# A transformer stack on one Trainium2 core: the neighbourhood attention's output projection in split form

## The chip, the cores and the metric

The program runs on one core of a Trainium2 chip, in one launch. The metric is the device time of that core in microseconds. Below, PE is the matmul engine (TensorE), DVE is VectorE, ACT is ScalarE, POOL is GpSimd, and SP is the queue that issues the weight loads.

## The reference, cut to what matters

A first block (S5 branch, gated branch, cross attention, feed-forward) is followed by a second one of two layers. Each of these layers has a mixer and a feed-forward part, dense in layer 0 and a mixture of eight experts in layer 1. 256 tokens, 1024 features. The change touches only the mixer, which is, cut down:

```python
def mixer_block(x, w_in, b_gate, rpb, sink, w_branch_na, w_branch_sw, w_out):
    proj = x @ w_in
    q_na, k_na, v_na, q_sw, k_sw, v_sw, gate_logits = jnp.split(proj, ...)
    y_na = neighbourhood_attention(q_na, k_na, v_na, rpb)      # 8 heads of 64
    y_sw = sliding_window_attention(rotary(q_sw), rotary(k_sw), v_sw, sink)   # 8 heads of 64
    y_na = y_na @ w_branch_na                                  # (256, 512) @ (512, 1024)
    y_sw = y_sw @ w_branch_sw
    g_na, g_sw = jnp.split(sigmoid(gate_logits + b_gate), 2, axis=-1)
    return (g_na * y_na + g_sw * y_sw) @ w_out
```

## The kernel before, in words

**Two forms of a matmul.** An fp32 product is one instruction in the program and two records in the trace. The split form writes each operand as a high part (rounded to fp32r by ACT) and a low part (operand minus high part, by DVE), and adds up three fp32r matmuls: high x high, high x low, low x high. Most weights are used in split form (`split_a`, L701, and `split_b`, L728). The two branch projections of a mixer, `bna` with the weight `w_na` and `bsw` with `w_sw`, are in fp32 by `form_a4` (L668), which reads the weights straight from the ring.

**Weights.** SP streams chunks of 128 x 2048 elements into a ring of 7 slots in the fixed order of `plan_chunks`; the first matmul of a chunk releases a slot (`chunk_used`). `split_plan` (L138) lists the chunks that are split and the PSUM unit each is used for. ACT makes the high part of the next one at each `wp_part` (L1362), DVE the low part at each `wp_rest` (L1819), into two buffers that alternate; part n waits until PE has finished the unit of part n-2. So the places of these calls in the two engines' programs are the schedule of the splits, written by hand.

**PSUM.** Every result is a unit in the list of `plan_units`, and unit n lies in bank n mod 8. PE opens a unit when the consumer of the unit eight before has freed that bank.

**The pair attention** (`pair_attention`: PE L771, ACT L1315, DVE L1781) handles 8 pairs of heads, 0 to 3 for the neighbourhood and 4 to 7 for the sliding window. The engines run it in step, each in program order, one iteration j per pair:
- PE: the scores of pair j+1 (L781), the eight transposes of pair j-1's probabilities (L794; they wait for `prob_ready` from DVE), half of a gate's projection (24 split matmuls, L709), and the output of pair j-1 (L806; it waits for ACT's copies of the transposes).
- ACT: the exponentials of pair j (L1327), two copies of pair j-1's transposes (L1335), at odd j a sigmoid gate (L1561) and one `wp_part` (L1372), and last the copy of output j-1 out of PSUM (L1341), which frees its unit. It goes to `onT` in region r_v for pairs 0 to 3 and to `osT` in r_zu for the others.
- DVE: bias and scale of pair j's scores (L1792), their maximum (L1796) and its negative (L1802), then the reciprocal of pair j-1's sums (L1810) and the product with it (L1812), which raises `prob_ready`; at j = 2, 4 and 6 one `wp_rest` (L1825).

Behind the loop PE runs four banks of `bna` and four of `bsw` (L675, eight products a bank), then the output projection from the merged and split sum (L721), for which it waits on DVE's L1830. DVE multiplies the banks of `bna` by the gate (L2161), those of `bsw` too (L2166), and adds them (L2170). ACT's `merged_high` (L1378) and DVE's `merged_rest` (L1830) split the sum. Mixer 0 is followed by the dense feed-forward part, mixer 1 by the experts.

Of the kernel before, what the change touches and what calls it, by code (L numbers as in the profile page):

```python
# [137 lines left out]
def split_plan():  # L138

    out = [((("k8", "w_" + n, i)), (n, i)) for n in ("out", "q", "xo") for i in range(4)]  # L140
    for m in range(2):
        units = [(f"projb{m}", i) for i in range(5)] + [(f"{n}{m}", i) for n in ("qk", "ga", "gb") for i in range(4)]
        out += [(("k8", f"w_in_{m}", i), unit) for i, unit in enumerate(units)]
        out += [(("k8", f"w_out_{m}", i), (f"out{m}", i) if i < 3 else (f"last{m}", TB - 1)) for i in range(4)]
    return out
# [102 lines left out]
def build(nc, a, out):  # L248
    with ExitStack() as ctx:
# [3 lines left out]
        def sem(name):  # L253
            return ctx.enter_context(nc.semaphore(name))
# [84 lines left out]
        def view(region, lo, size, pat, **kw):  # L339
            return region[:, lo:lo + size].rearrange(pat, **kw)  # L340
# [50 lines left out]
        v_na = view(r_v, 0, 1024, "p (b d) -> p b d", b=TB)  # L391
        onT = view(r_v, 1024, 1024, "p (k t) -> p k t", t=TOK)
        qsT = view(r_k, 0, 1024, "p (k t) -> p k t", t=TOK)
# [43 lines left out]
        m_split = sem("m_split")  # L437
        hf_high = sem("hf_high")
        acc_free = sem("acc_free")
        qk_roped = sem("qk_roped")  # L440
# [43 lines left out]
        def free_unit(last, u):  # L484
            last.then_inc(bank_free[UNIT_AT[u] % BANKS], 1)
# [137 lines left out]
        def _(pe):  # L623
# [70 lines left out]

            def split_chunk(chunk):

                n = SPLIT_AT[chunk]
                pe.wait_ge(wp_split, n + 1)
                return [w.rearrange("p (k c) -> p k c", k=KD) for w in wp_slot(n)]

# [323 lines left out]
            for m in range(2):  # L1024
# [45 lines left out]
                for c in range(2):  # L1070
                    form_a4(f"bna{m}", ("k4", f"w_na_{m}", c), onT, 2 * c)
                evacuated(pe, (f"at{m}_o", PAIR_N - 1))
# [172 lines left out]
        def _(act):  # L1245
# [69 lines left out]
            def pair_attention(name, dst_of, sink_of, between):  # L1315
                g0 = head0[name]
                for j in range(PAIR_N + 1):
# [20 lines left out]
                    if j >= 1:  # L1338
                        u = (name + "_o", j - 1)
                        take_unit(act, u)  # L1340
                        free_unit(nc.scalar.activation(dst_of(j - 1), bank(u)[:, 0:TOK], ACT.Copy), u)  # L1341

# [185 lines left out]
            for m in range(2):  # L1528
# [47 lines left out]
                def gate_b(j):  # L1576

                    if j < PAIR_N and j % 2 == 1:
                        gate(f"gb{m}", j // 2, gbT, 8)
                        wp_part()  # L1580

                pair_attention(f"at{m}", lambda j: (onT if j < 4 else osT)[:, j % 4, :],
                               lambda i: sink_col(m, i - 8) if i >= 8 else None, gate_b)
                merged_high(4 + 4 * m)
                for _ in range(2):
# [82 lines left out]
        def _(dve):  # L1668
# [111 lines left out]

            def pair_attention(name, bias_of, sink_of):  # L1781
                g0 = head0[name]
                for j in range(PAIR_N + 1):
                    if j < PAIR_N:
# [12 lines left out]
                        if sink_of(2 * j) is not None:  # L1797
# [3 lines left out]
                            link(last)  # L1801
                        V.tensor_scalar(negm[:, j % 2, :], mx[:, j % 2, :], -1.0, None, ALU.mult).then_inc(negm_ready, 1)  # L1802
                    if j >= 1:
                        g = g0 + j - 1
# [327 lines left out]
            for m in range(2):  # L2132
# [18 lines left out]
                for _ in range(7):  # L2151
                    wp_rest()
                dve.wait_ge(loads["nab"], 16 * (m + 1))
                pair_attention(f"at{m}", lambda i: nabias[:, i, :, :] if i < 8 else swmask,
                               lambda i: sink_col(m, i - 8) if i >= 8 else None)
                wp_rest()
                evacuated(dve, (f"gb{m}", 3))
                for i in range(4):
                    take_unit(dve, (f"bna{m}", i))
                    gs = gaT[:, 2 * i:2 * i + 2, :]  # L2160
                    last = V.tensor_tensor(gs, gs, halves(bank((f"bna{m}", i))), ALU.mult)  # L2161
                    free_unit(last, (f"bna{m}", i))
                for i in range(4):
                    take_unit(dve, (f"bsw{m}", i))
# [315 lines left out]
```

## Time and profile before

| | |
|---|---|
| median of 3 runs | 2272.61 us (2268.06 to 2275.58) |
| the profiled execution | 2271.9 us |
| its span, first to last instruction | 2270.1 us |
| PE busy | 94% |
| PE weight loads busy | 83% |
| DVE busy | 69% |
| ACT busy | 53% |
| mean granted clock of PE | 0.972 |

The two pair attentions lie at 704 to 763 us (mixer 0) and 1113 to 1173 us (mixer 1), and the branch projections behind each take some 28 us. PE's records overlap one another, so the cost of a matmul in a row of equal ones is read from start to start, not from its duration. The bracket at the end of a timeline row is the idle time of the engine before it, and who ended it.

### The profile page before, as it was taken

The page shows a single profiled execution, that of the slowest core. Times are in us where ns is not written, and L with a number is a line of the kernel's source. Part 1 is how long each engine was busy: PE and PEld are TensorE (multiplying, and loading weights), DVE is VectorE, ACT ScalarE, POOL GpSimd, SP SyncE. Part 2 cuts the span into 40 slices and gives each one's busy share as a digit, 9 for nine tenths or more (in the row PEclk, how much of TensorE's full clock was granted, in tenths as well). Part 3 has the DMA queues.
Part 4 walks back from the last instruction along what each step waited for, and adds up shares of the span by engine and source line. Part 5 has one row for each costly group of instructions (what it writes and reads, how often), then busy time and mean ns, then how long its engine had stood idle before and what let it go on. Part 6 is the DMA issues. An engine that isn't in the chain of part 4 may idle for free.

```text
span 2270.1 us, 33147 instructions
## 1 busy us (share of the span) xinstructions
PE 2142.9 (94%) x12590; PEld 1875.5 (83%) x12590; DVE 1572.9 (69%) x1749; ACT 1195.3 (53%) x1215; POOL 9.8 (0%) x22
## 2 busy tenths in 40 slices
PE   7999988899898889998988999999999999999997
PEld 7888877799797789998877788888888888888885
DVE  8677343544636454454555888989898989899897
ACT  3200233333437433343552677777777777677774
POOL 0000000000000000000000000000000000000000
PEclk9999989899999989999998899999999999999998
DMA  7343432355463245555323698989898989989884
GB/s 300 140 149 111 147 117 97 122 186 185 157 246 117 93 149 186 186 186 201 134 89 116 271 371 344 367 345 367 341 365 341 367 350 362 371 336 370 351 357 161
DMA packets 76446, 542.02 MB, mean 239 GB/s; under 512 B 9152, under 2 KB 9296, under 8 KB 11968
## 3 DMA queue, kind: packets, MB, share of 16 engines
q1 hardware_dynamic: 72144, 524.32, 59.9%
q0 software_dynamic: 2080, 10.40, 1.2%
q10 hardware_dynamic: 2128, 5.93, 0.7%
q8 instruction: 73, 1.20, 0.2%
q14 instruction: 21, 0.17, 0.0%
HBM read 539.57 MB, written 1.05 MB: 238 GB/s over the span
## 4 chain that ended last, share of the span: by engine, by line
PE 88%; DVE 5%; ACT 4%; issue 1%; DMA 0%; DVEq 0%; ACTq 0%
PE psum L1178 13%; PE psum L822 11%; PE psum L1155 9%; PE psum L1159 9%; PE psum L1158 9%; PE psum L662 7%; PE psum L721 6%; PE psum L709 6%; PE psum L835 4%; PE psum L675 3%; PE psum L688 2%; PE psum L1121 2%; PE psum L1167 1%; ACT wp_h L1372 1%; PE psum L979 1%
## 5 line engine op out<-in xcount | busy, mean ns | idle before, releaser
L2210 DVE TENSOR_TENSOR w_l<-ring,w_h 128x2048 fp32r<-128x2048 f32 x338 | 773.2, 2290 | 115.5 <-ACT w_h L1358 108.9
L1358 ACT ACTIVATE w_h<-ring 128x2048 fp32r<-128x2048 f32 x338 | 647.5, 1916 | 138.9 <-PE psum L1155 95.4
L1155 PE MATMUL psum<-w_h,xe_h 128*128 128x512 f32 x896 | 359.8, 402 | 2.4 <-DVE xe_l L2294 2.4
L1159 PE MATMUL psum<-w_h,xe_l 128*128 128x512 f32 x896 | 350.6, 391 | 0.0
L1158 PE MATMUL psum<-w_l,xe_h 128*128 128x512 f32 x896 | 350.2, 391 | 0.0
L1851 DVE TENSOR_TENSOR wf_l<-ring,wf_h 128x2048 fp32r<-128x2048 f32 x66 | 151.2, 2291 | 156.5 <-ACT wf_h L1349 156.5
L1825 DVE TENSOR_TENSOR wp_l<-ring,wp_h 128x2048 fp32r<-128x2048 f32 x52 | 119.1, 2291 | 163.8 <-ACT wp_h L1372 163.8
L822 PE MATMUL psum<-xf_h,wf_h 128*128 128x256 f32 x704 | 200.9, 285 | 4.3 <-DVE xf_l L1843 2.4
L822 PE MATMUL psum<-xf_l,wf_h 128*128 128x256 f32 x704 | 200.6, 285 | 0.0
L822 PE MATMUL psum<-xf_h,wf_l 128*128 128x256 f32 x704 | 200.5, 285 | 0.0
L1155 PEld LDWEIGHTS psum<-w_h,xe_h 128*128 128x128 f32 x896 | 168.6, 188 | 38.2 <-DVE w_l L2210 3.9
L1159 PEld LDWEIGHTS psum<-w_h,xe_l 128*128 128x128 f32 x896 | 168.6, 188 | 36.2
L1158 PEld LDWEIGHTS psum<-w_l,xe_h 128*128 128x128 f32 x896 | 169.1, 189 | 32.3
L1349 ACT ACTIVATE wf_h<-ring 128x2048 fp32r<-128x2048 f32 x66 | 125.9, 1910 | 113.9 <-PE psum L835 58.5
L1372 ACT ACTIVATE wp_h<-ring 128x2048 fp32r<-128x2048 f32 x52 | 99.4, 1914 | 148.1 <-PE psum L721 78.3
L822 PEld LDWEIGHTS psum<-xf_h,wf_h 128*128 128x128 f32 x704 | 136.5, 194 | 5.8 <-DVE xf_l L1843 2.8
L1178 PE MATMUL psum<-w_h,eT_h 128*128 128x512 f32 x448 | 140.0, 394 | 0.0
L721 PE MATMUL psum<-wp_h,xf_h 128*128 128x256 f32 x384 | 114.5, 298 | 25.8 <-DVE xf_l L1859 12.9
L1178 PE MATMUL psum<-w_h,eT_l 128*128 128x512 f32 x448 | 138.4, 390 | 0.0
L1178 PE MATMUL psum<-w_l,eT_h 128*128 128x512 f32 x448 | 138.3, 390 | 0.0
L822 PEld LDWEIGHTS psum<-xf_l,wf_h 128*128 128x128 f32 x704 | 136.7, 194 | 0.7
L822 PEld LDWEIGHTS psum<-xf_h,wf_l 128*128 128x128 f32 x704 | 136.6, 194 | 0.0
(371 smaller groups left out, 3713.1 us busy)
## 6 DMA issues: line engine op xcount, KB each, us to landing
ring<-in_stream SPq DMA_DIRECT2D x499, 1024.0 KB, 5.8
big<-in_bc POOLq DMA_DIRECT2D x11, 512.0 KB, 7.6
big<-in_na_bias POOLq DMA_DIRECT2D x2, 2048.0 KB, 8.8
h<-in_x SPq DMA_DIRECT2D x2, 512.0 KB, 4.2
big<-in_mem ACTq DMA_DIRECT2D x1, 1024.0 KB, 12.2
big<-in_s_c ACTq DMA_DIRECT2D x1, 1024.0 KB, 13.2
r_k<-in_sgu_ln ACTq DMA_DIRECT2D x1, 1024.0 KB, 17.8
out_dram<-ysum ACTq DMA_DIRECT2D x1, 1024.0 KB, 4.0
```

The source lines that it names most:

```text
L662: last = nc.tensor.matmul(bank(unit)[:, j * TOK:(j + 1) * TOK], w[:, k, j * P:(j + 1) * P], act_T[:, k, :], start=(k == 0), stop=(k == KD ...
L709: last = nc.tensor.matmul(bank(unit)[:, j * TOK:(j + 1) * TOK], w[:, k, j * P:(j + 1) * P], x[:, k, :], start=(k == i == 0), stop=(k == KD ...
L721: last = nc.tensor.matmul(bank(unit)[:, at * 256:(at + 1) * 256], x[:, k, b * P:(b + 1) * P], w[:, k, :], start=(k == i == 0), stop=(k == ...
L822: last = nc.tensor.matmul(psum[:, ff_bank(name, b), j * TOK:(j + 1) * TOK], w[:, k, j * P:(j + 1) * P], x[:, k, :], start=(k == i == 0), s ...
L1155: first = nc.tensor.matmul(out, xe_h[:, k, :], wh[:, i, :], start=(k == 0), stop=False)
L1158: nc.tensor.matmul(out, xe_h[:, k, :], wl[:, i, :], start=False, stop=False)
L1159: last = nc.tensor.matmul(out, xe_l[:, k, :], wh[:, i, :], start=False, stop=(k == KD - 1))
L1178: last = nc.tensor.matmul(psum[:, 4 + c, :], x[:, s % 2, k, :], w[:, k, c * 512:(c + 1) * 512], start=(s == 0 and k == n == 0), stop=(s == ...
L1349: nc.scalar.activation(wf_h[:, n % SPLITS, :], ring[:, at % SLOTS, :], ACT.Copy).then_inc(wf_high, 1)
L1358: nc.scalar.activation(high, src, ACT.Copy).then_inc(w_high, 1)
L1851: V.tensor_tensor(wf_l[:, n % SPLITS, :], ring[:, at % SLOTS, :], wf_h[:, n % SPLITS, :].bitcast(F32), ALU.subtract).then_inc(wf_split, 1)
L2210: V.tensor_tensor(low, src, high.bitcast(F32), ALU.subtract).then_inc(w_split, 1)
```

## The change

- `bna` goes through the new `split_a4`, three fp32r matmuls for each fp32 product, on the split weight `w_na` and the split attention output. `split_plan` gets the two chunks of `w_na` behind those of the gates.
- The attention output of pairs 0 to 3 is split where it leaves PSUM: ACT's copy now writes the high part `on_h` (in a free half slot of `wf_l`) and raises `on_high`; DVE's new `on_rest` takes the low part `on_l` (in `hf_l`) from the same PSUM unit, and frees the unit instead of ACT.
- `on_rest` for pair j-2 stands in DVE's iterations j = 2 to 5, behind the negated maximum and before the reciprocal of pair j-1.
- ACT makes two more weight parts per mixer behind the loop and before `merged_high`. DVE makes the two low parts behind the second and the fourth bank of `bna`.

```diff
--- before.py
+++ after.py
@@ -141,6 +141,7 @@
     for m in range(2):
         units = [(f"projb{m}", i) for i in range(5)] + [(f"{n}{m}", i) for n in ("qk", "ga", "gb") for i in range(4)]
         out += [(("k8", f"w_in_{m}", i), unit) for i, unit in enumerate(units)]
+        out += [(("k4", f"w_na_{m}", c), (f"bna{m}", 2 * c + 1)) for c in range(2)]
         out += [(("k8", f"w_out_{m}", i), (f"out{m}", i) if i < 3 else (f"last{m}", TB - 1)) for i in range(4)]
     return out
 
@@ -389,7 +390,8 @@
         qnT = view(r_zu, 0, 1024, "p (k t) -> p k t", t=TOK)
         knT = view(r_zu, 1024, 1024, "p (k t) -> p k t", t=TOK)
         v_na = view(r_v, 0, 1024, "p (b d) -> p b d", b=TB)
-        onT = view(r_v, 1024, 1024, "p (k t) -> p k t", t=TOK)
+        on_h = wf_l[:, 1, 1024:2048].rearrange("p (k t) -> p k t", t=TOK)
+        on_l = hf_l.rearrange("p a b t -> p (a b) t")
         qsT = view(r_k, 0, 1024, "p (k t) -> p k t", t=TOK)
         ksT = r_k[:, 1024:1280]
         v_sw = view(r_k, 1280, 256, "p (b d) -> p b d", b=TB)
@@ -436,6 +438,7 @@
         wp_split = sem("wp_split")
         m_split = sem("m_split")
         hf_high = sem("hf_high")
+        on_high = sem("on_high")
         acc_free = sem("acc_free")
         qk_roped = sem("qk_roped")
         rexp_in = sem("rexp_in")
@@ -692,11 +695,26 @@
                             release(last, chunk)
                 close_unit(last, unit)
 
-            def split_chunk(chunk):
+            def split_chunk(chunk, k=KD):
 
                 n = SPLIT_AT[chunk]
                 pe.wait_ge(wp_split, n + 1)
-                return [w.rearrange("p (k c) -> p k c", k=KD) for w in wp_slot(n)]
+                return [w.rearrange("p (k c) -> p k c", k=k) for w in wp_slot(n)]
+
+            def split_a4(name, chunk, x_h, x_l, u0):
+
+                wh, wl = split_chunk(chunk, 4)
+                for u in range(2):
+                    open_unit(pe, (name, u0 + u))
+                    for j in range(2):
+                        at = slice((2 * u + j) * P, (2 * u + j + 1) * P)
+                        for k in range(4):
+                            for i, (w, x) in enumerate(((wh, x_h), (wh, x_l), (wl, x_h))):
+                                last = nc.tensor.matmul(bank((name, u0 + u))[:, j * TOK:(j + 1) * TOK], w[:, k, at],
+                                                        x[:, k, :], start=(k == i == 0), stop=(k == 3 and i == 2))
+                                if i == u == j == k == 0:
+                                    release(last, chunk)
+                    close_unit(last, (name, u0 + u))
 
             def split_a(unit, chunk, tiles=(0, 1)):
 
@@ -1068,7 +1086,7 @@
                                half_gate)
                 evacuated(pe, (f"at{m}_o", 3))
                 for c in range(2):
-                    form_a4(f"bna{m}", ("k4", f"w_na_{m}", c), onT, 2 * c)
+                    split_a4(f"bna{m}", ("k4", f"w_na_{m}", c), on_h, on_l, 2 * c)
                 evacuated(pe, (f"at{m}_o", PAIR_N - 1))
                 for c in range(2):
                     form_a4(f"bsw{m}", ("k4", f"w_sw_{m}", c), osT, 2 * c)
@@ -1338,7 +1356,11 @@
                     if j >= 1:
                         u = (name + "_o", j - 1)
                         take_unit(act, u)
-                        free_unit(nc.scalar.activation(dst_of(j - 1), bank(u)[:, 0:TOK], ACT.Copy), u)
+                        last = nc.scalar.activation(dst_of(j - 1), bank(u)[:, 0:TOK], ACT.Copy)
+                        if j - 1 < 4:
+                            last.then_inc(on_high, 1)
+                        else:
+                            free_unit(last, u)
 
             def wf_part(name, n):
 
@@ -1579,8 +1601,10 @@
                         gate(f"gb{m}", j // 2, gbT, 8)
                         wp_part()
 
-                pair_attention(f"at{m}", lambda j: (onT if j < 4 else osT)[:, j % 4, :],
+                pair_attention(f"at{m}", lambda j: (on_h if j < 4 else osT)[:, j % 4, :],
                                lambda i: sink_col(m, i - 8) if i >= 8 else None, gate_b)
+                for _ in range(2):
+                    wp_part()
                 merged_high(4 + 4 * m)
                 for _ in range(2):
                     wp_part()
@@ -1778,7 +1802,15 @@
                     if i >= 2:
                         xf_rest_of((name + "_o", i - 2), "x_o", i - 2)
 
-            def pair_attention(name, bias_of, sink_of):
+            def on_rest(m, j):
+
+                u = (f"at{m}_o", j)
+                take_unit(dve, u)
+                dve.wait_ge(on_high, 4 * m + j + 1)
+                last = V.tensor_tensor(on_l[:, j, :], bank(u)[:, 0:TOK], on_h[:, j, :].bitcast(F32), ALU.subtract)
+                free_unit(last, u)
+
+            def pair_attention(name, bias_of, sink_of, mixer):
                 g0 = head0[name]
                 for j in range(PAIR_N + 1):
                     if j < PAIR_N:
@@ -1800,6 +1832,8 @@
                                 last = V.tensor_scalar(m, m, sink_of(2 * j + hd), None, ALU.max)
                             link(last)
                         V.tensor_scalar(negm[:, j % 2, :], mx[:, j % 2, :], -1.0, None, ALU.mult).then_inc(negm_ready, 1)
+                    if 2 <= j < 6:
+                        on_rest(mixer, j - 2)
                     if j >= 1:
                         g = g0 + j - 1
                         dve.wait_ge(exp_ready, g + 1)
@@ -2152,7 +2186,7 @@
                     wp_rest()
                 dve.wait_ge(loads["nab"], 16 * (m + 1))
                 pair_attention(f"at{m}", lambda i: nabias[:, i, :, :] if i < 8 else swmask,
-                               lambda i: sink_col(m, i - 8) if i >= 8 else None)
+                               lambda i: sink_col(m, i - 8) if i >= 8 else None, m)
                 wp_rest()
                 evacuated(dve, (f"gb{m}", 3))
                 for i in range(4):
@@ -2160,6 +2194,8 @@
                     gs = gaT[:, 2 * i:2 * i + 2, :]
                     last = V.tensor_tensor(gs, gs, halves(bank((f"bna{m}", i))), ALU.mult)
                     free_unit(last, (f"bna{m}", i))
+                    if i % 2 == 1:
+                        wp_rest()
                 for i in range(4):
                     take_unit(dve, (f"bsw{m}", i))
                     gs = gbT[:, 2 * i:2 * i + 2, :]
```

In the rows of the program below, `hf_l<-psum,wf_l` is `on_rest`. This is DVE in mixer 0 before, iterations 2 and 3 of the pair attention:

```order
L1792 SCALAR_TENSOR_TENSOR r_zv<-psum,big 128x512 x2
L1796 TENSOR_REDUCE mx<-r_zv 128x4
L1802 TENSOR_SCALAR negm<-mx 128x4
L1810 RECIPROCAL rsum<-ssum 128x4
L1812 TENSOR_TENSOR uT<-uT,rsum 128x1024
L1825 TENSOR_TENSOR wp_l<-ring,wp_h 128x2048
L1792 SCALAR_TENSOR_TENSOR uT<-psum,big 128x512 x2
L1796 TENSOR_REDUCE mx<-uT 128x4
L1802 TENSOR_SCALAR negm<-mx 128x4
L1810 RECIPROCAL rsum<-ssum 128x4
```

and now:

```order
L1824 SCALAR_TENSOR_TENSOR r_zv<-psum,big 128x512 x2
L1828 TENSOR_REDUCE mx<-r_zv 128x4
L1834 TENSOR_SCALAR negm<-mx 128x4
L1810 TENSOR_TENSOR hf_l<-psum,wf_l 128x256
L1844 RECIPROCAL rsum<-ssum 128x4
L1846 TENSOR_TENSOR uT<-uT,rsum 128x1024
L1859 TENSOR_TENSOR wp_l<-ring,wp_h 128x2048
L1824 SCALAR_TENSOR_TENSOR uT<-psum,big 128x512 x2
L1828 TENSOR_REDUCE mx<-uT 128x4
L1834 TENSOR_SCALAR negm<-mx 128x4
L1810 TENSOR_TENSOR hf_l<-psum,wf_l 128x256
L1844 RECIPROCAL rsum<-ssum 128x4
```

One subtraction more stands in each of iterations 2 to 5, between the negated maximum and the reciprocal. The rest of the order is the same.

DVE behind mixer 0's pair attention, before:

```order
L1812 TENSOR_TENSOR uT<-uT,rsum 128x1024
L1825 TENSOR_TENSOR wp_l<-ring,wp_h 128x2048
L2161 TENSOR_TENSOR r_ga<-r_ga,psum 128x512 x4
L2166 TENSOR_TENSOR r_gb<-r_gb,psum 128x512
L2170 TENSOR_TENSOR r_ga<-r_ga,r_gb 128x512
```

and now (L1859 is `wp_rest`, L2195 the multiplication of a bank of `bna` by the gate, L2202 that of `bsw`):

```order
L1846 TENSOR_TENSOR uT<-uT,rsum 128x1024
L1859 TENSOR_TENSOR wp_l<-ring,wp_h 128x2048
L2195 TENSOR_TENSOR r_ga<-r_ga,psum 128x512 x2
L1859 TENSOR_TENSOR wp_l<-ring,wp_h 128x2048
L2195 TENSOR_TENSOR r_ga<-r_ga,psum 128x512 x2
L1859 TENSOR_TENSOR wp_l<-ring,wp_h 128x2048
L2202 TENSOR_TENSOR r_gb<-r_gb,psum 128x512
L2206 TENSOR_TENSOR r_ga<-r_ga,r_gb 128x512
```

The four multiplications of `bna` are now in twos, each two with a low part of an output weight behind it. The low part ahead of them belongs to `w_na` now, and to an output weight before.

ACT from the last output copy on, before:

```order
L1335 ACTIVATE r_zv<-psum 128x512 x2
L1341 ACTIVATE r_zu<-psum 128x256
L1378 ACTIVATE xf_h<-r_ga 128x512 x4
L1372 ACTIVATE wp_h<-ring 128x2048 x2
L1262 ACT_TABLE_LOAD
```

and now (L1400 is `merged_high`):

```order
L1353 ACTIVATE r_zv<-psum 128x512 x2
L1359 ACTIVATE r_zu<-psum 128x256
L1394 ACTIVATE wp_h<-ring 128x2048 x2
L1400 ACTIVATE xf_h<-r_ga 128x512 x4
L1394 ACTIVATE wp_h<-ring 128x2048 x2
L1280 ACT_TABLE_LOAD
```

Two high parts have come in ahead of `merged_high`.

## Rows read from the trace of the kernel before

**Rows 1.** The page, parts 1 and 4: busy time by engine; the chain by engine.
```profile
PE 2142.9 (94%) x12590; PEld 1875.5 (83%) x12590; DVE 1572.9 (69%) x1749; ACT 1195.3 (53%) x1215; POOL 9.8 (0%) x22
...
PE 88%; DVE 5%; ACT 4%; issue 1%; DMA 0%; DVEq 0%; ACTq 0%
```

**Rows 2.** Waits of PE, 1110 to 1205: us in total, times, longest us.
```profile
PE psum L806 <- ACT r_zv L1335: 7.1, 4, 2.2
...
PE psum L721 <- DVE xf_l L1830: 2.9, 1, 2.9
```

**Rows 3.** Timeline of DVE, mixer 1's neighbourhood projection: start, us, operation, idle before.
```profile
1180.88 0.69 DVE L2161 TENSOR_TENSOR r_ga<-r_ga,psum 128x512 f32<-128x512 f32 x1 [2.69 <-PE psum L675]
...
1187.78 0.69 DVE L2161 TENSOR_TENSOR r_ga<-r_ga,psum 128x512 f32<-128x512 f32 x1 [2.76 <-PE psum L675]
```

**Rows 4.** Timeline of PE in mixer 1's pair attention.
```profile
1126.92 1.14 PE L781 MATMUL psum<-r_zu 64*128 64x256 f32 x8
1127.98 1.09 PE L794 MATMUL psum<-ident,uT 128*128 128x128 f32 x8
1128.83 0.36 PE L709 MATMUL psum<-xf_h,wp_h 128*128 128x256 f32 x1
1129.04 0.28 PE L709 MATMUL psum<-xf_l,wp_h 128*128 128x256 f32 x1
...
1131.66 0.28 PE L709 MATMUL psum<-xf_h,wp_l 128*128 128x256 f32 x1
1133.38 1.08 PE L806 MATMUL psum<-r_zv,r_v 128*64 128x256 f32 x8 [1.44 <-ACT r_zv L1335]
...
1135.46 0.76 PE L794 MATMUL psum<-ident,r_zv 128*128 128x128 f32 x5
...
1141.51 0.76 PE L794 MATMUL psum<-ident,uT 128*128 128x128 f32 x5
...
1147.19 1.08 PE L806 MATMUL psum<-r_zv,r_v 128*64 128x256 f32 x8 [1.73 <-ACT r_zv L1335]
...
1149.27 0.98 PE L794 MATMUL psum<-ident,r_zv 128*128 128x128 f32 x7
...
1171.15 1.98 PE L806 MATMUL psum<-r_zv,r_k 128*64 128x256 f32 x8 [2.23 <-ACT r_zv L1335]
```

**Rows 5.** Timeline of DVE, last output projection: 128x256 operation that reads PSUM.
```profile
1226.49 0.42 DVE L2190 SCALAR_TENSOR_TENSOR h<-h,psum 128x256 f32<-128x256 f32 x1 [1.94 <-PE psum L721]
```

**Rows 6.** Timeline of DVE in mixer 1's pair attention, iteration 2.
```profile
1125.80 0.17 DVE L1810 RECIPROCAL rsum<-ssum 128x4 f32<-128x4 f32 x1
1126.01 1.22 DVE L1812 TENSOR_TENSOR uT<-uT,rsum 128x1024 f32<-128x1024 f32 x1
1128.68 2.29 DVE L1825 TENSOR_TENSOR wp_l<-ring,wp_h 128x2048 fp32r<-128x2048 f32 x1 [1.46 <-ACT wp_h L1372]
1130.89 1.28 DVE L1792 SCALAR_TENSOR_TENSOR uT<-psum,big 128x512 f32<-128x512 f32 x2
```

**Rows 7.** Timeline of ACT in mixer 1's pair attention.
```profile
1126.74 1.91 ACT L1372 ACTIVATE wp_h<-ring 128x2048 fp32r<-128x2048 f32 x1
1128.54 0.38 ACT L1341 ACTIVATE r_v<-psum 128x256 f32<-128x256 f32 x1
...
1134.50 0.39 ACT L1341 ACTIVATE r_v<-psum 128x256 f32<-128x256 f32 x1 [1.22 <-PE psum L806]
...
1141.99 0.38 ACT L1341 ACTIVATE r_v<-psum 128x256 f32<-128x256 f32 x1
```

**Rows 8.** Windows around two gaps of PE; the column behind POOL is the granted clock.
```profile
700.00:704.50 4.50, 1.52 (x14) 1.30 (x13) 2.03 (x1) 3.95 (x7) 0.00 (x0) 1.00 0.00 0
704.50:707.00 2.50, 2.48 (x20) 2.17 (x21) 1.53 (x3) 1.22 (x1) 0.00 (x0) 1.00 0.03 7
1109.60:1113.10 3.50, 0.51 (x7) 0.30 (x5) 2.07 (x1) 3.48 (x7) 0.00 (x0) 0.97 0.00 0
1113.10:1116.50 3.40, 3.40 (x16) 2.69 (x16) 1.49 (x3) 1.17 (x1) 0.00 (x0) 0.53 0.00 0
```

## The prediction

> **What bounds the kernel.** I began with the page's busy shares and its chain. TensorE (PE) is busy 94% of the span and carries 88% of the chain that ended last [rows 1]: a microsecond taken from PE counts in full, and so does a microsecond by which PE is made to wait. Then I asked what PE waits for in mixer 1's attention and projections [rows 2], and read that stretch on PE, VectorE (DVE) and ScalarE (ACT). Mixer 0 has the same schedule to within some tenths of a microsecond, so each term counts twice. PE's waits in the pair attention are for ACT's copies of the transposed probabilities, 7.1 us in four pieces, and one of 2.9 us stands before the output projection. The attention is thus a loop in which PE, DVE and ACT hand work round with little to spare. The change makes one projection cheaper on PE, and puts one more step into that loop.
>
> **1. The projection.** DVE takes one finished bank of it every 3.45 us (1180.88 to 1187.78 is two banks) [rows 3]. A bank holds 8 products of 128x128 by 256 columns, so one fp32 product costs 3.45 / 8 = 0.431 us. In the split form it is three matmuls; 23 of these start between 1129.04 and 1131.66, so 2.62 / 22 = 0.119 us each [rows 4], and 24 in a bank are 2.87 us. The gain is 0.58 us a bank, over four banks and two mixers **-4.6 us**, all of it on the path.
> By these rows an fp32 product costs 3.6 split matmuls. The Trainium skill (FP8 and Floating Point Precision, "TensorE Precision Notes") counts four passes for true fp32. With four the gain would be 64 x 0.119 = 7.6 us, and the sum 3 us lower; the rows decide.
>
> **2. The low half of each output, on DVE.** New in DVE's pair iterations 2 to 5 is a subtraction that waits for the output unit of pair j-2 and for ACT's copy of it. It stands in front of the reciprocal and the product that PE needs for its next transposes. DVE runs in order, so they wait too. For its own length I take the 0.42 us of the 128x256 row from PSUM [rows 5]; the bounds are the reciprocal's 0.17 [rows 6] and the 0.69 of twice the width [rows 3].
> - *Iteration 2.* Today the reciprocal starts at 1125.80, the product at 1126.01 and ends at 1127.23 [rows 6], and PE transposes at 1127.98, right behind the scores of 1126.92 [rows 4]. ACT's copy of output 0 comes only behind a gate and a 1.91 us weight split: 1128.54 + 0.38 = 1128.92 [rows 7]. The subtraction then runs to 1129.35, reciprocal and product take 0.21 + 1.22 = 1.43, and PE transposes at 1130.8: 2.8 late. PE idles from the end of the scores, 1128.06, for 2.7 us.
> - *Iteration 3.* PE's gate half starts 0.85 behind the transposes and lasts 24 x 0.12 = 2.9 us, so output 1 starts at 1134.6 instead of 1133.38, where it had waited 1.44 for ACT [rows 4]: part of the delay is swallowed. ACT's copy starts 1.12 behind (1134.50 today [rows 7]), ends near 1136.15, and with 0.42 + 1.43 the product is ready at 1138.0. PE transposes then, not at 1135.46 [rows 4]: 2.6 late. DVE's own scores work starts 2.0 late (behind the rest that followed the product) and would be ready before.
> - *Iteration 4.* All is 2.6 late on arrival. ACT's copy of output 2, again behind a gate and a split, ends at 1141.99 + 0.38 + 2.6 = 1145.0 [rows 7]; + 1.85 gives 1146.85. The transposes come there instead of at 1141.51 [rows 4]: 5.3 late.
> - *Iteration 5.* Output 3 starts at 1146.85 + 0.85 + 2.9 = 1150.6 where it was 1147.19 after 1.73 of waiting; copied 1152.1, transposes near 1154.0 to 1154.5 instead of 1149.27 [rows 4]: 5.0 late, 5.2 as middle.
>
> The last four iterations have no subtraction and run as today. They don't win the delay back, since PE, ACT and DVE have all been pushed by it. So **+5.2 us per mixer, +10.4 us**. With 0.17 in place of 0.42 in four serial places it is 2.0 less over both mixers, with 0.69 it is 2.2 more.
>
> **3. Two more splits per mixer, 1.91 on ACT and 2.29 on DVE each** [rows 6, 7]. During the attention their number is the same as now: the last two split the neighbourhood weights where the first two output weights were split. Those come behind the second and the fourth projection bank. DVE sits idle 2.7 us before every bank there [rows 3]. Behind the fourth bank ACT and DVE need 1.9 + 2.3 = 4.2 us, and the next bank is full after 3.45, so DVE takes it 0.8 late; a bank of the second projection costs DVE some 2.1 of its 3.45 us, so it has caught up one bank on. PE needs the first of these weights only after four such banks and 2.9 us more. Cost **0**; were that cover gone, it would be at most 2.3 us per mixer before the output projection.
>
> **4. Banks, ring, queues: 0.** An output's bank is freed by DVE, some 3 us later than by ACT, and is opened again eight units on. No DMA is issued; the ring's slots are released by the same first matmuls in the same order, and the weights now read early lie before those that were read at that time. SP only shifts with PE.
>
> **5. The clock.** PE now idles 2.7 us before the transposes of pairs 1 and 3, four times over both mixers. Idle PE has been followed by the lower level in these rows, though not always: 0.51 busy of 3.50 and then a granted clock of 0.53 over the next 3.4 us; the same gap in mixer 0 (1.52 of 4.50), then 1.00 [rows 8]; 2.23 us idle before the last output, whose eight records then took 1.98 where others take 1.08 [rows 4]. At the lower level (1.2 instead of 2.4 GHz) PE does half, so a stretch of 3.4 us costs up to 1.7 us, and here it falls on transposes, gate and output, which are on the path. Bounds are 0 and 4 x 1.7 = 6.8; I take two of four: **+3.4 us**. The Trainium skill (TensorE: Matmul & The Clock Gate, "HAM oscillation — how this bites in real kernels") warns only of gaps longer than these. By it this term is 0 and the sum +5.8; the row with 2.23 us idle speaks against it.
>
> **Sum:** -4.6 + 10.4 + 0 + 0 + 3.4 = **+9.2 us**. On the profiled execution's 2271.9 us that gives 2281.1; the median of the runs is 0.7 higher, within their spread of 7.5. I say 2281.
>
> **Rivals.**
> - *A, the forecast:* DVE's in-order wait plus one or more clock drops, 2281 (+7.5 with one, +12.6 with four).
> - *B, the same wait, the clock stays up:* +5.8, 2277.7. For it: the gap of some 3 us in mixer 0 did no harm. Against: the same gap in mixer 1, and one of 2.23, did. 0.3% is 6.8 us here, about what a measurement of this kernel can tell from no change, so this counts as no change.
> - *C, the splits behind the projection aren't covered:* DVE falls behind in the second projection, and PE's 2.9 us wait before the output projection [rows 2] grows by up to 2.3 per mixer: 2281 + 4.6 = 2286. Against it are DVE's 2.7 us gaps.
> - *D, the other side, the copy is there in time:* if ACT had output j-2 copied when DVE gets there, the subtraction would cost DVE 0.42 where it has slack, and the -4.6 would stand alone: 2267.3. It decides at 1125.8, and the copy lands at 1128.92, 3.1 too late; output 1's lands at 1134.88, and the transposes of 1135.46 need DVE to begin its last 1.43 us by 1134.0. To be faster by over 0.3% the fp32 products would also have to cost more than measured.
>
> **How the numbers follow.** Chances: A 0.57, B 0.29, C 0.06, D 0.08. Slower by over 0.3% is A and C, 0.63; within 0.3% is B and most of D, 0.34; faster 0.03. The range goes from B less the spread of a median, some 3 us, to four clock drops (2284.5) with the longer subtraction and the same spread: 2275 to 2289.
>
> **What would show it.** In the changed profile: DVE idle before the subtraction, ended by ACT's copy, about 3 us in iterations 2 and 4 and less in 3 and 5; PE idle before the transposes of pairs 1 and 3 near 2.7 us, ended by DVE's product; scores of pair 0 to the first projection matmul 5 us longer; projection banks 2.87 us apart, not 3.45; the wait before the output projection still 2.9. I am wrong if DVE finds the copy done, if the later iterations win back the delay, or if the output projection waits longer.

## The result, and the profile after

The changed kernel takes 2279.57 us (median of 6 runs, 2277.97 to 2283.92). The kernel before, run beside it, takes 2273.15 us (6 runs). The ratio is 1.0035, with a 95% interval of 1.0019 to 1.0051: slower by 6.4 us in the medians, 8 us by the ratio. The profiled execution is the slowest of the six, 2283.92 us with a span of 2282.1, against 2271.9 and 2270.1 before. So the two traces lie 12 us apart, more than the medians do, and some of that has to be something that isn't in every execution.

The page's busy times, and its chain by engine (compare [rows 1]):

```profile
PE 2144.2 (94%) x12654; PEld 1879.3 (82%) x12654; DVE 1585.2 (69%) x1761; ACT 1202.9 (53%) x1219; POOL 9.8 (0%) x22
...
PE 89%; DVE 6%; ACT 3%; issue 1%; DMA 0%; DVEq 0%; ACTq 0%
```

PE is busy 1.3 us more, though its work has become less, and DVE 12.3 us more. Nothing here tells where 12 us went. The waits of PE in mixer 1 do (us in total, times, longest; compare [rows 2]):

```profile
PE psum L812 <- DVE uT L1846: 5.5, 2, 2.8
PE psum L812 <- DVE r_zv L1846: 4.9, 4, 1.5
PE psum L824 <- ACT r_zv L1353: 4.0, 2, 2.2
PE psum L799 <- issue: 3.0, 1, 3.0
PE psum L739 <- DVE xf_l L1864: 2.9, 1, 2.9
```

L812 are the transposes, L824 the outputs, L739 the output projection. PE waited 7.1 us for ACT's copies before the outputs, and it waits 4.0 now. In their place come 10.4 us of waiting for DVE's product before the transposes, where the kernel before had 2.0:

```profile
PE psum L794 <- DVE r_zv L1812: 2.0, 2, 1.2
```

So PE waits 8.4 us more for DVE and 3.1 less for ACT, 5.3 in all. The wait before the output projection is 2.9 us, as it was.

DVE's timeline in mixer 1's loop, iteration 2 whole and the subtraction (L1810) of the next three (compare [rows 6]):

```profile
1134.83 0.17 DVE L1834 TENSOR_SCALAR negm<-mx 128x4 f32<-128x4 f32 x1
1138.13 0.42 DVE L1810 TENSOR_TENSOR hf_l<-psum,wf_l 128x256 fp32r<-128x256 f32 x1 [3.14 <-ACT wf_l L1359]
1138.47 0.17 DVE L1844 RECIPROCAL rsum<-ssum 128x4 f32<-128x4 f32 x1
1138.68 1.22 DVE L1846 TENSOR_TENSOR uT<-uT,rsum 128x1024 f32<-128x1024 f32 x1
...
1145.46 0.42 DVE L1810 TENSOR_TENSOR hf_l<-psum,wf_l 128x256 fp32r<-128x256 f32 x1 [0.70 <-ACT wf_l L1359]
...
1154.30 0.42 DVE L1810 TENSOR_TENSOR hf_l<-psum,wf_l 128x256 fp32r<-128x256 f32 x1 [2.74 <-ACT wf_l L1359]
...
1163.10 0.43 DVE L1810 TENSOR_TENSOR hf_l<-psum,wf_l 128x256 fp32r<-128x256 f32 x1 [1.78 <-ACT wf_l L1359]
```

The subtraction of iteration 2 stands idle 3.14 us until ACT has copied the output, and reciprocal and product stand behind it. At 1134.83 the negated maximum was out; before, the reciprocal followed that at once [rows 6]. In iterations 3, 4 and 5 the wait is 0.70, 2.74 and 1.78 us. The long ones are the even iterations, where ACT had a gate and a weight part ahead of the copy. PE's timeline, the transposes of pairs 1 to 4 (compare [rows 4]):

```profile
1139.96 1.09 PE L812 MATMUL psum<-ident,uT 128*128 128x128 f32 x8 [2.79 <-DVE uT L1846]
...
1147.29 1.09 PE L812 MATMUL psum<-ident,r_zv 128*128 128x128 f32 x8 [1.29 <-DVE r_zv L1846]
...
1156.12 1.97 PE L812 MATMUL psum<-ident,uT 128*128 128x128 f32 x8 [2.72 <-DVE uT L1846]
...
1165.12 1.09 PE L812 MATMUL psum<-ident,r_zv 128*128 128x128 f32 x8 [1.49 <-DVE r_zv L1846]
```

PE idles 2.79 us before pair 1 and 2.72 before pair 3. The eight transposes of pair 3 take 1.97 us instead of 1.09. The granted clock, in the column behind POOL, says why (windows from the transposes of pairs 1 and 3 on; compare [rows 8]):

```profile
1139.90:1143.90 4.00, 3.94 (x34) 3.81 (x34) 3.96 (x5) 2.48 (x9) 0.00 (x0) 1.00 0.27 92
1156.20:1159.70 3.50, 3.50 (x18) 3.50 (x19) 3.47 (x4) 2.72 (x10) 0.00 (x0) 0.55 0.26 35
```

Both gaps are equally long. Behind the first the clock stays at its upper level, behind the second it is at the lower one (0.55 in a window that holds the end of the stretch too).

The projection itself has become what was forecast. The first of these two rows is a matmul of it, the second the one 43 matmuls later: 5.16 / 43 = 0.120 us each, 2.88 us a bank where a bank took 3.45 [rows 3].

```profile
1195.72 0.28 PE L713 MATMUL psum<-hf_l,wp_h 128*128 128x256 f32 x1
...
1200.88 0.28 PE L713 MATMUL psum<-wf_l,wp_l 128*128 128x256 f32 x1
```

With that the 12 us between the two traces are accounted for. The pair attention, from the first transposes of pair 0 to those of pair 7, takes 55.6 us in mixer 0 and 52.5 in mixer 1, where it took 45.8 in both: 16.5 us more. The projections give back 4.6.

### The profile page after: what moved, and what is told of

It reads as the page before. It is cut to its first block, busy times and chain, and to the rows that moved or that the text cites. A ratio compares the mean times of both kernels' runs of the same rounds, so it can differ in the third digit from the quotient of the medians.

```text
span 2282.1 us, 33303 instructions
## 1 busy us (share of the span) xinstructions
PE 2144.2 (94%) x12654; PEld 1879.3 (82%) x12654; DVE 1585.2 (69%) x1761; ACT 1202.9 (53%) x1219; POOL 9.8 (0%) x22
## 4 chain that ended last, share of the span: by engine, by line
PE 89%; DVE 6%; ACT 3%; issue 1%; DMA 0%; DVEq 0%; ACTq 0%
PE psum L1196 13%; PE psum L840 11%; PE psum L1173 9%; PE psum L1177 9%; PE psum L1176 9%; PE psum L665 7%; PE psum L727 7%; PE psum L739 6%; PE psum L853 4%; PE psum L691 3%; PE psum L678 2%; PE psum L1139 2%; PE psum L713 1%; PE psum L1185 1%; ACT wp_h L1394 1%
## 5 line engine op out<-in xcount | busy, mean ns | idle before, releaser
L1859 DVE TENSOR_TENSOR wp_l<-ring,wp_h 128x2048 fp32r<-128x2048 f32 x56 | 128.2, 2291 | 164.1 <-ACT wp_h L1394 164.1
L1394 ACT ACTIVATE wp_h<-ring 128x2048 fp32r<-128x2048 f32 x56 | 107.1, 1914 | 168.6 <-PE psum L739 78.2
L739 PE MATMUL psum<-wp_h,xf_h 128*128 128x256 f32 x384 | 114.6, 298 | 25.9 <-DVE xf_l L1893 13.1
```

Source lines behind the costliest of these rows:

```text
L739: last = nc.tensor.matmul(bank(unit)[:, at * 256:(at + 1) * 256], x[:, k, b * P:(b + 1) * P], w[:, k, :], start=(k == i == 0), stop=(k == ...
L1394: nc.scalar.activation(wp_slot(n)[0], ring[:, at % SLOTS, :], ACT.Copy).then_inc(wp_high, 1)
```

## The experiments

Each ratio to the kernel before has its 95% interval. Beside them stands the length of the pair attention, over the 45.8 us that it takes before. Three series ran, e1 to e4, e5 to e8, and e9 with e10, the last on another chip, each with its own runs of the kernel before (medians 2269.86, 2272.32 and 2272.15 us). The last two columns are read from the one profiled execution of each kernel, the ratios from all of its runs. "Low" is the time in that stretch for which the granted clock was at its lower level.

| kernel | median, us | ratio | loop, mixer 0 / 1, over 45.8 us | low, mixer 0 / 1 |
|---|---|---|---|---|
| changed | 2279.57 | 1.0035 (1.0019 to 1.0051) | +9.8 / +6.7 | 10.2 / 3.4 |
| e1, changed again | 2284.77 | 1.0060 (1.0040 to 1.0080) | +9.5 / +9.4 | 10.2 / 10.2 |
| e2, subtraction last | 2268.14 | 0.9985 (0.9972 to 0.9998) | +0.1 / +0.1 | 0 / 0 |
| e3, subtraction alone | 2292.07 | 1.0084 (1.0061 to 1.0108) | +9.8 / +9.5 | 10.2 / 10.2 |
| e4, PE filled | 2279.24 | 1.0038 (1.0027 to 1.0050) | +5.2 / +6.6 | 0 / 3.4 |
| e5, wait only | 2279.32 | 1.0033 (1.0022 to 1.0045) | +6.6 / +5.4 | 6.8 / 3.4 |
| e6, copy first | 2277.00 | 1.0023 (1.0010 to 1.0037) | +5.6 / +4.0 | 3.4 / 0 |
| e7, changed again | 2280.79 | 1.0041 (1.0026 to 1.0057) | +6.7 / +6.7 | 3.4 / 3.4 |
| e8, both split | 2267.96 | 0.9986 (0.9973 to 1.0000) | +0.4 / +0.4 | 0 / 0 |
| e9, e2 again | 2267.55 | 0.9981 (0.9971 to 0.9992) | +3.0 / +0.1 | 6.8 / 0 |
| e10, both split, later | 2266.82 | 0.9974 (0.9963 to 0.9986) | +0.4 / +0.4 | 0 / 0 |

**The changed kernel again.**

> The changed kernel once more, for comparison with the other kernels of this series. Theory W (the subtraction makes DVE wait for ACT's copy ahead of the product that PE needs, +5.2 us per mixer; the projection gives back 2.3; clock drops add what they will): +6 to +10 us over the kernel before, four waits of DVE ahead of the subtraction per mixer, projection banks 2.87 us apart. Rival L (DVE has simply more work: two subtractions' worth and two low parts per mixer): the same total, but the waits would stand elsewhere.

It came out at 1.0060, 13.6 us by the ratio, over the +10 that I had put as the end. Both loops held the subtraction's wait and 10.2 us at the lower clock. In mixer 1 the clock was at its lower level in both of these windows, that is through the transposes of pair 1 and most of the gate half behind them:

```profile
1135.80:1138.50 2.70, 2.70 (x13) 2.70 (x14) 2.70 (x3) 2.52 (x8) 0.00 (x0) 0.50 0.00 0
1138.60:1141.40 2.80, 2.80 (x15) 2.80 (x15) 1.91 (x3) 0.00 (x0) 0.00 (x0) 0.50 0.68 252
```

**The subtraction's place.** e2 changes this alone:

```diff
-                    if 2 <= j < 6:
-                        on_rest(mixer, j - 2)
                     if j >= 1:
...
                     if j in (2, 4, 6):
                         wp_rest()
+                    if 2 <= j < 6:
+                        on_rest(mixer, j - 2)
```

> Only the place of the subtraction changes: it comes last in DVE's iteration, behind the product and behind the low part of a weight. All the work of the change is still done. Theory W: PE's transposes of pairs 1 to 4 come when they did before the change, 0.1 to 0.3 us late at the end of the loop, the 2.3 us per mixer of the projection are left as gain: -4 us against the kernel before (-3 to -4.6), -10 us against the changed kernel. Rival L (it is the amount of DVE's work): no more than 1 or 2 us better than the changed kernel. Rival K (clock drops make most of the loss): drops as many as in the changed kernel, and no more than 3 us better.

Measured 0.9985, 3.4 us under the kernel before by the ratio (1.7 by the medians), and 16.6 us under e1 in the same series. Against the changed kernel 10 us were expected; it is more because e1 came out slower than I had put it. The loops are as long as before the change to 0.1 us, with all four subtractions in them. On DVE, iteration 2 in mixer 1:

```profile
1126.21 0.17 DVE L1834 TENSOR_SCALAR negm<-mx 128x4 f32<-128x4 f32 x1
1126.29 0.17 DVE L1842 RECIPROCAL rsum<-ssum 128x4 f32<-128x4 f32 x1
1126.49 1.23 DVE L1844 TENSOR_TENSOR uT<-uT,rsum 128x1024 f32<-128x1024 f32 x1
1129.18 2.29 DVE L1859 TENSOR_TENSOR wp_l<-ring,wp_h 128x2048 fp32r<-128x2048 f32 x1 [1.46 <-ACT wp_h L1394]
1131.39 0.42 DVE L1810 TENSOR_TENSOR hf_l<-psum,wf_l 128x256 fp32r<-128x256 f32 x1
```

Reciprocal and product follow the negated maximum at once again. The subtraction comes behind the low part of the weight, for which DVE waits anyway, and finds the copy done: no bracket on its row, nor on the other seven of the two mixers. And PE's transposes of pair 1 stand without a wait:

```profile
1128.48 1.09 PE L812 MATMUL psum<-ident,uT 128*128 128x128 f32 x8
```

That takes away both the amount of DVE's work (rival L) and the two weight parts more as causes, since e2 does all of it. The banks that DVE frees in place of ACT are out as well, since e2 keeps that too. It can't say how the loss divides between the wait and the clock, which both went.

**The subtraction alone,** in the kernel before, with the projection in fp32. The low half is computed and not read, and DVE frees the bank behind ACT's copy, as in the change. The line that matters:

```diff
+                    if 2 <= j < 6:
+                        on_rest(mixer, j - 2)
                     if j >= 1:
                         g = g0 + j - 1
```

> The kernel before with the subtraction and its waits in the loop, and the projection still in fp32; the low half is written and never read. Theory W: +5.2 us per mixer, +10.4 us in all and up to 3.4 more for clock drops: 10 to 14 us over the kernel before, and 4.6 over the changed kernel. Rival D (the copy is there in time, the loss comes from the split projection and its two late weight splits): at most 1 or 2 us over the kernel before.

Measured 1.0084: 19 us over the kernel before by the ratio, and 7.3 over e1 by the medians, where 4.6 were expected. The loops are those of e1, 9.8 and 9.5 us longer, and DVE waits as long in iteration 2 as in the changed kernel:

```profile
1138.74 0.42 DVE L1793 TENSOR_TENSOR hf_l<-psum,r_v 128x256 fp32r<-128x256 f32 x1 [3.14 <-ACT r_v L1342]
```

So the whole loss sits in the loop, and the split projection is a gain. The 19 us are more than the 10 to 14 forecast because 20.4 us of the loops ran at the lower clock. The 2.7 us between 7.3 and 4.6 are within what the two intervals, each some 0.2% either way, leave open.

**The clock by itself.** e4 keeps PE busy in the two gaps and leaves DVE's wait as it is:

```diff
+                        if j in (2, 4):
+                            open_unit(pe, (name + "_t", 2 * j - 2))
+                            for _ in range(22):
+                                nc.tensor.transpose(bank((name + "_t", 2 * j - 2))[:, 0:P], ident[:, :], ident[:, :])
                         pe.wait_ge(prob_ready, g + 1)
```

> The changed kernel with 22 transposes of the identity on PE (some 2.4 us) ahead of PE's wait for the product in iterations 2 and 4, into the bank that is opened next. PE is busy where it idled for 2.7 us, and the wait itself stays. Theory W with its clock term: no stretch at the lower clock between the first gate half and the last output of the loop; the delay per mixer is 5.2 us, and the time 0 to 7 us under that of the changed kernel, by 1.7 for each drop that the changed kernel has. If the drops don't matter: the same time as the changed kernel within 0.5 us.

PE in iteration 2 of mixer 1, the filler and then the transposes:

```profile
1131.33 2.62 PE L809 MATMUL psum<-ident 128*128 128x128 f32 x22
1134.19 1.09 PE L816 MATMUL psum<-ident,uT 128*128 128x128 f32 x8 [0.24 <-DVE uT L1850]
```

Windows behind both gaps of that loop:

```profile
1134.20:1138.00 3.80, 3.80 (x32) 3.75 (x32) 3.77 (x4) 2.42 (x8) 0.00 (x0) 1.00 0.35 99
1150.40:1154.00 3.60, 3.60 (x31) 3.60 (x32) 3.57 (x4) 2.76 (x10) 0.00 (x0) 1.00 0.30 68
```

The gap is down to 0.24 us, and behind both the clock is 1.00, where in e1 it was 0.50. The loop of mixer 0 held no low stretch at all and is 5.2 us longer than before: this is the price of the subtraction and its wait without the clock. In mixer 1 one stretch remained, but late, at pair 6, where the kernel before has its gaps too, and it cost 1.3 us. The time fell by 5.5 us against e1, in this series; against the kernel before, e4 (1.0038) is no better than the changed kernel was in the first comparison (1.0035) or in e7 (1.0041), so how much the filler gains beside a typical execution is not shown. I had expected no low stretch in either loop.

What the gaps do can be counted over all traces. The changed kernel, e1, e3 and e7 have 16 gaps of 2.7 to 2.8 us before the transposes of pairs 1 and 3, and at 13 of them the clock fell to its lower level in the gap or within some 1 us of its end; in e5, with gaps of 2.4 us, it did at 3 of 4. At the four filled gaps of e4 it never did, nor at the four places in e6, where the gap is 1.2 to 1.3 us, nor at the 20 in the kernel before, e2, e8, e9 and e10, which have no gap there.

**Wait or work.** In e5 DVE waits at the old place, and subtracts behind the product:

```diff
                     if 2 <= j < 6:
-                        on_rest(mixer, j - 2)
+                        take_unit(dve, (f"at{mixer}_o", j - 2))
+                        dve.wait_ge(on_high, 4 * mixer + j - 1)
...
+                    if 2 <= j < 6:
+                        on_rest(mixer, j - 2)
                     if j in (2, 4, 6):
```

> DVE waits for the output and ACT's copy at the old place, ahead of the reciprocal, and does the subtraction behind the product. Theory W splits the loss in two: the wait alone shifts the projection by 3.9 us per mixer, the four subtractions of 0.42 us by the other 1.3 to 1.4. So some 2.6 us under the changed kernel, 3 to 8 over the kernel before. Rival (the subtractions' own time is most of the loss): more than 6 us under the changed kernel.

With one low stretch of 3.4 us the loop is +5.4 (mixer 1), and the changed kernel's is +6.7 with one (e7): 1.3 us less, as forecast for the 0.42 us of four subtractions. The other 3.9 of the 5.2 are the wait. In the medians it was 1.5 us, not 2.6. The profiled execution had 6.8 us of low clock in mixer 0 here and 3.4 in e7, which may be why; single executions can't show it.

**The copy's place on ACT.** e6 moves `wp_part` from behind the gate to behind the output's copy, at odd steps:

```diff
                         gate(f"gb{m}", j // 2, gbT, 8)
-                        wp_part()
...
                             free_unit(last, u)
+                    if j < PAIR_N and j % 2 == 1:
+                        wp_part()
```

> The changed kernel with one thing moved on ACT: at odd steps the output's copy goes ahead of the 1.91 us high part of a weight. If the copy's place behind that part is what makes the wait long, DVE's wait in iterations 2 and 4 falls from 3.1 and 2.7 us to some 1.6 and 1.2, and those iterations end 1.5 us sooner each; a part of it is lost again, since the low part of the weight then comes later, and 1.2 us per mixer are left: 2 to 3 us under the changed kernel. If it is the output itself that is late (PE), the wait stays and the time too.

DVE's wait in iteration 2 falls from 3.14 to 1.63 us, and PE's gap from 2.79 to 1.29:

```profile
1130.58 0.42 DVE L1811 TENSOR_TENSOR hf_l<-psum,wf_l 128x256 fp32r<-128x256 f32 x1 [1.63 <-ACT wf_l L1359]
```

```profile
1132.40 1.09 PE L812 MATMUL psum<-ident,uT 128*128 128x128 f32 x8 [1.29 <-DVE uT L1847]
```

Mixer 1 is +4.0 without a low stretch, just as 5.2 - 1.2. The time is 3.8 us under e7, a little more than the 2 to 3 expected. No low stretch followed a gap of 1.3 us here. So it is ACT's order, the weight part ahead of the copy, that made the even iterations the long ones.

**The changed kernel in this series.**

> The changed kernel again, in the same series as the two variants above. Theory W gives +5.8 without a clock drop and 1.7 more for each: so far +8 and +14 in two series; 8 to 14 expected, with 2 to 6 drops more than the kernel before in the loops, and the time moving with their number.

1.0041, or 9.3 us, with one low stretch of 3.4 us in each loop, both behind the gap before pair 3. Over e1, e7 and the first comparison the loss goes 13.6, 9.3 and 8 us, and the loops of the profiled executions held 20.4, 6.8 and 13.6 us at the lower level. The single execution need not be like the median of its series, so the order of the last two says nothing.

**A better version.** e8 and e10 split the sliding window's projection too, on top of e2, with the subtractions of pairs 4 to 7 and two more weight parts per mixer:

```diff
-                    form_a4(f"bsw{m}", ("k4", f"w_sw_{m}", c), osT, 2 * c)
+                    split_a4(f"bsw{m}", ("k4", f"w_sw_{m}", c), os_h, os_l, 2 * c)
...
                     if i >= 1:
                         merged_rest(f"out{m}", i - 1)
+                    if i == 1:
+                        wp_rest()
                 merged_rest(f"out{m}", 3)
+                wp_rest()
```

> A version that may beat both: the subtraction last in DVE's iteration, and the sliding window's projection in split form too, with its own subtractions in the last four iterations and two more weight parts per mixer. PE gains another 4 banks x 0.58 us per mixer, -4.6 more. Against it stand a low part of a weight (2.29) between the banks of the second projection, where DVE has 2.87 us a bank and 2.1 of work, which leaves the last bank some 0.7 late, and the last subtraction. Expected 1 to 4 us under the version with only the subtraction moved, -4 to -8 against the kernel before; if DVE becomes the bound before the output projection, PE's wait there grows from 2.9 us to more than 5.2 and nothing is gained.

It was no faster than e2 (0.9986 against 0.9985). PE's wait before the output projection, and DVE's row behind the second bank:

```profile
PE psum L742 <- DVE xf_l L1867: 5.2, 1, 5.2
```

```profile
1193.51 2.29 DVE L1862 TENSOR_TENSOR wp_l<-ring,wp_h 128x2048 fp32r<-128x2048 f32 x1 [1.90 <-ACT wp_h L1394]
```

PE gained 4.6 us more on the path and waits 2 x 2.3 us more: the rival of that expectation. The two loops are 0.4 us longer each besides. DVE idles 1.90 us for ACT's high part at 1193.51, with a full bank waiting behind it. e10 puts this low part one bank later (`i == 2`).

> The version with both projections in split form, with the low part of the first output weight one bank later on DVE. There it waited 1.9 us for ACT's high part, with a full bank behind it, and PE waited 5.2 us before the output projection. One bank later the high part is done, and the last bank is taken some 1.2 us late instead of 2.3: PE's wait falls from 5.2 to about 4.2 us, 2 us over both mixers, and the time to some 5 us under the kernel before. If the wait stays at 5 us, it is DVE's amount of work in that stage and not the place.

```profile
PE psum L742 <- DVE xf_l L1867: 4.1, 1, 4.1
```

```profile
1193.53 2.28 DVE L1862 TENSOR_TENSOR wp_l<-ring,wp_h 128x2048 fp32r<-128x2048 f32 x1
```

The idle time on DVE is gone and PE's wait is down to 4.1 us in both mixers. e10 takes 2266.82 us, 0.9974: 5.9 us under the kernel before by the ratio, the furthest of all versions, though the intervals of e2 and e9 end under 1 too. e2 ran beside it:

> The version with only the subtraction moved, again, beside the one below: 2 to 5 us under the kernel before, as in the first series (ratio 0.9985).

0.9981, so e10 leads it by 0.7 us in the medians; the intervals overlap, and which of the two is the faster stays open. One cost of e8 and e10 was left out of their expectations: in both, the lower clock level lasts 6.8 us around the start of the output projection, in both mixers, and 3.4 us in e2 and the kernel before.

e9 also warns about the last column. Its loop of mixer 0 holds two low stretches and is 3.0 us longer, with no new gap at all. The first of them:

```profile
717.40:720.70 3.30, 3.30 (x18) 3.30 (x17) 3.20 (x6) 1.88 (x3) 0.00 (x0) 0.50 0.00 0
```

It follows PE's wait of 1.9 us before the transposes of pair 0, which the kernel before has as well. The same place has a low stretch in mixer 0 of the changed kernel's trace and of e3, and none in the kernel before. So some 1.5 us of that +9.8 aren't shown to be the change's.

## Why the prediction was right, point by point

**The time.** 2281 was forecast, between 2275 and 2289, slower by over 0.3% with 0.63; measured were 2279.57 and +0.35%. The interval, 0.19% to 0.51%, holds 0.3%, so on which side of it this comparison came out is partly luck; e1 and e7 give +0.60% and +0.41%. The mechanism was the one named: the wait, and lower-clock stretches behind its gaps.

**1, the projection.** Right to 0.01 us: 0.119 us a matmul by the rows, 0.120 measured (24 x 0.119 is 2.86 us and not 2.87, which changes nothing). What it brings alone shows in e2, where nothing else is left of the change in mixer 1's loop: 4.6 us on the path forecast, 3.4 and 4.3 by the two ratios (0.9985 and 0.9981), with intervals that hold 4.6. With the four passes for true fp32 of the Trainium skill (FP8 and Floating Point Precision, "TensorE Precision Notes") it would have been 7.6 us, a ratio of 0.9967; the intervals end at 0.9972 and 0.9971, so the measured row was the better guide.

**2, the wait.** Right, in size and shape. Iteration by iteration, from the start of mixer 1's loop, the transposes of pairs 1, 2 and 3 come 2.9, 2.7 and 5.5 us late (1139.96, 1147.29 and 1156.12, less 1122.17, against 1127.98, 1135.46 and 1141.51, less 1113.07); forecast were 2.8, 2.6 and 5.3. For pair 4 the low clock comes in; e4 has none in that place and the loop of its mixer 0 is +5.2 in the end, the number of the forecast. The last four iterations win nothing back. That the end number fits to 0.1 us is in part luck: the working for pair 4 gave 1154.0 to 1154.5 less 1149.27, that is 4.7 to 5.2 late, and the upper end went into the sum as its middle.

**3 and 4, splits, banks, ring.** Right at 0: the wait before the output projection is 2.9 us with the two more weight parts. e8 shows where that cover ends: with two parts more, a low part came between the banks of the second projection, and PE's wait grew by 2.3 us per mixer.

**5, the clock.** The term was the uncertain one and stayed so. The direction was right: 13 of 16 such gaps were followed by the lower level and none of the four filled ones in e4, which was 5.5 us faster than e1. The Trainium skill (TensorE: Matmul & The Clock Gate, "HAM oscillation — how this bites in real kernels") warns only of longer gaps and would have given 0 here; these runs disagree. Two of four falls at 1.7 us each was the guess; behind the new gaps the traces show three of four in the changed kernel, four in e1 and e3, and two in e7. A stretch of 3.4 us costs 1.5 (from +5.2 to +6.7), a little less than put down; but it can last 6.8, which I hadn't allowed for, and a loop can hold three, the first ahead of any new gap. The worst loops lost 4.6 us to it, so the bound of 6.8 us for both mixers was too low: e1 has 8.4. The first comparison lies 0.6 us over the sum without a fall by the medians and 2.2 by the ratio, while its profiled execution, the slowest of the six, lost 6.1 us to the lower level, 1.5 of them ahead of any new gap. By their loops, e7's trace lost 3.0 us and e1's 8.4, so the 3.4 us of the forecast stand at the lower end; what an average execution loses to the clock was not measured apart.

**Rivals.** B (the wait, no falls) would have been +5.8 us, 2277.7. The first comparison's +6.4 by the medians is nearer to that than to A's +9.2, its +8.0 by the ratio nearer to A. The traces decide: all three of the changed kernel have falls at the new gaps, so B's condition did not hold in them. e1 and e7 are nearer to A by either. C and D are out: C by the 2.9 us wait, D by the bracket of 3.14 us.

## What to carry to other kernels

In a loop in which several engines hand work round, look for each new instruction not only at its own length but at what stands behind it on an in-order engine: 0.42 us of subtraction cost 2.8, because of the wait in front of it, and nothing at all when it stood behind the product. Put such work behind the last thing that another engine waits for, best where the engine is going to wait for the same producer anyway. And where two calls of a producer (here ACT's copy and its weight part) serve consumers of different urgency, the urgent one goes first.

## What the runs showed of the hardware that I had not expected

- Gaps of PE of 2.7 to 2.8 us were followed by the lower clock 13 times in 16, and not always in the same execution; gaps of 1.2 to 1.3 us in the same places of e6 were not. A gap of 1.9 us before pair 0 of mixer 0 was followed by it in the changed kernel, e3 and e9, and not in the kernel before. Filling each of the four gaps with 22 transposes whose result is thrown away took 5.5 us off e1 in the first series.
- The lower level lasted 3.4 us after most gaps, and 6.8 us in e1 and in e3. In e1 the gate half went on at 0.213 us a matmul instead of 0.120 until 1141.4. A stretch of 3.4 us costs 1.3 to 1.6 us of loop, and 10.2 us of it in one loop cost 4.2 to 4.6.
- The same kernel lost 13.6, 9.3 and 8 us to the kernel before in three series, with intervals of 0.2% either way. What sets which gap is followed by a fall is not shown by these runs.
